# Norm boundaries cut into five token tiles, keys and queries of attention staged under the last projection, three mixing chunks split under the last attention unit

## What is computed

```python
def trunk_layer(x, mod, g_mix_pre, g_mix_post, g_ffn_pre, g_ffn_post, w_ffn_in, w_ffn_conv, w_ffn_out, mixer):
    shift1, scale1, gate1, shift2, scale2, gate2 = mod      # six vectors, silu(c) @ w_mod + b_mod
    h = rmsnorm(x, g_mix_pre) * (1 + scale1) + shift1
    y, ctx_state = mixer(h)                                  # w_in, heads, w_out
    x = x + gate1 * rmsnorm(y, g_mix_post)
    h = rmsnorm(x, g_ffn_pre) * (1 + scale2) + shift2
    x = x + gate2 * rmsnorm(conv_ffn(h, w_ffn_in, w_ffn_conv, w_ffn_out), g_ffn_post)
    return x, ctx_state
```

## Time and profile before

| what | us |
|---|---|
| three runs, median | 1647.64 |
| three runs, lowest and highest | 1643.89, 1649.33 |
| profiled execution, its own time | 1646.06 |
| profiled execution, span | 1644.3 |
| PE busy | 1555.4 (95% of the span) |
| VectorE busy | 1087.6 (66%) |
| ScalarE busy | 700.5 (43%) |
| GpSimd busy | 117.2 (7%) |

### The profile page before, as it was taken

One profiled execution on the slowest core, in us unless ns is written; L12 is line 12 of the kernel. 1 busy time (PEld: TensorE's weight loads), 2 busy tenths in 40 slices (PEclk: granted clock), 3 DMA queues, 4 the chain that ended last, 5 costly groups with the idle time before them and its releaser, 6 DMA issues.

```text
span 1644.3 us, 27983 instructions
## 1 busy us (share of the span) xinstructions
PE 1555.4 (95%) x10553; PEld 1414.5 (86%) x10553; DVE 1087.6 (66%) x2082; ACT 700.5 (43%) x1263; POOL 117.2 (7%) x128
## 2 busy tenths in 40 slices
PE   6799898989999999999989989989899999999997
PEld 2699687879998789998779988768799988999986
DVE  5598766888777867778884248872866641466544
ACT  6631666354443234443252237662644432344332
POOL 1250220000000000000010032410000000000000
PEclk8799899999999999999989989999999999999999
DMA  8234101613334763334642220102222222222222
GB/s 328 105 115 129 33 2 59 211 52 105 113 115 147 217 174 115 115 105 168 198 135 69 75 81 2 44 4 76 61 82 77 70 71 89 73 70 76 70 81 92
DMA packets 45953, 164.54 MB, mean 100 GB/s; under 512 B 5584, under 2 KB 6608, under 8 KB 45104
## 3 DMA queue, kind: packets, MB, share of 16 engines
q1 hardware_dynamic: 42336, 152.00, 28.5%
q0 software_dynamic: 2320, 10.54, 2.0%
q10 hardware_dynamic: 1216, 0.92, 0.2%
HBM read 159.87 MB, written 3.57 MB: 99 GB/s over the span
## 4 chain that ended last, share of the span: by engine, by line
PE 81%; DVE 7%; DMA 2%; issue 2%; ACT 1%; ACTq 0%; DVEq 0%; SPq 0%
PE ps L1842 22%; PE ps L1843 22%; PE ps L1943 13%; PE ps L1935 6%; PE ps L2100 4%; PE ps L2129 4%; PE ps L2042 3%; PE ps L2115 3%; DMA work<-in_wmodt 2%; DVE work L1081 1%; PE ps L1867 1%; PE ps L2034 1%; PE ps L2116 1%; PE ps L2134 1%; DVE product L1081 1%
## 5 line engine op out<-in xcount | busy, mean ns | idle before, releaser
L1842 PE MATMUL ps<-hh,whi 128*128 128x320 f32 x864 | 268.4, 311 | 7.7 <-DVE wlo L1067 3.8
L1842 PE MATMUL ps<-hh,wlo 128*128 128x320 f32 x864 | 267.7, 310 | 0.0
L1843 PE MATMUL ps<-hh,wlo 128*128 128x320 f32 x864 | 267.6, 310 | 0.0
L1842 PE MATMUL ps<-hl,whi 128*128 128x320 f32 x864 | 267.6, 310 | 0.0
L1843 PE MATMUL ps<-hl,whi 128*128 128x320 f32 x864 | 267.6, 310 | 0.0
L1843 PE MATMUL ps<-hh,whi 128*128 128x320 f32 x864 | 267.6, 310 | 0.0
L618 ACT ACTIVATE whi<-raw 128x1024 fp32r<-128x1024 f32 (+1 forms) x112 | 117.0, 1046 | 319.8 <-PE ps L1843 286.8
L612 ACT ACTIVATE whi<-raw 128x1024 fp32r<-128x1024 f32 (+1 forms) x70 | 72.1, 1033 | 264.3 <-PE ps L1943 173.6
L1943 PE MATMUL ps<-whi,ffh 128*128 128x512 f32 x440 | 171.9, 391 | 3.4 <-DVE wlo L1067 2.6
L1067 DVE TENSOR_TENSOR wlo<-raw,whi 128x1024 fp32r<-128x1024 f32 (+1 forms) x72 | 87.5, 1216 | 131.8 <-ACT whi L612 128.6
L1943 PE MATMUL ps<-wlo,ffh 128*128 128x512 f32 x440 | 171.3, 389 | 0.0
(11 more groups left out here) (226 smaller groups left out, 2897.8 us busy)
## 6 DMA issues: line engine op xcount, KB each, us to landing
raw<-in_w SPq DMA_DIRECT2D x174, 512.0 KB, 3.5
work<-in_wmodt SPq DMA_DIRECT2D x56, 512.0 KB, 3.6
ring<-in_wmodt SPq DMA_DIRECT2D x24, 512.0 KB, 4.3
work<-in_wmod SPq DMA_DIRECT2D x16, 512.0 KB, 6.8
grow<-gate_rows POOLq DMA_DIRECT2D x4, 1024.0 KB, 5.8
work<-in_rpb POOLq DMA_DIRECT2D x8, 448.0 KB, 4.5
x<-in_x SPq DMA_DIRECT2D x5, 512.0 KB, 7.9
out_x<-x SPq DMA_DIRECT2D x5, 512.0 KB, 2.6
```

The costliest lines, as they stand in the source:

```text
L1842: T.matmul(bankA[s], slot(w, s, k), h[:, k, 0:HT], start=st, stop=sp_)
L1843: last = T.matmul(bankB[s], slot(w, s, k), h[:, k, HT:NT], start=st, stop=sp_)
```

## The change

Four groups of edits.

1. **Boundaries.** `affine` is called for halves of four chunks, spread over VectorE and ScalarE by two tables. `boundary` becomes `mix_boundary` and `fout1_boundary`; PE turns three tiles and then multiplies tile by tile: ten pieces, five tiles of 128 tokens by two slots. `piece` waits only for its own slot and tile. The hand-written orders of ScalarE and VectorE change with it.
2. **Entries of attention.** Layer 0: the two value units are multiplied one after the other, each over four of the eight k chunks (`value_half` in place of `pair_v`; the host lays the weights out for it); the pooling products stand earlier (`pool_out`); the first keys are split before the last unit, the second ones (`second_keys`) after the first two units' maxima. Layer 1: the last projection signals at k == 3 (`s_free`), and keys and queries are staged from there; VectorE's next low weights stand inside attention. The buffers of the keys are laid out anew.
3. **Start of mixing.** The first three of eight chunks are split (`mix_in_hi`, `mix_in_low`) once all scores are done; the third tile of PE's first chunk waits for the last unit's output.
4. **Chunk loads.** Loads of modulation chunks 24 to 79 move from SP's queue to GpSimd's, with semaphores `s_mlate`; the second `spread_gate` stands behind the load of chunk 55 in that queue.

```diff
 
 
 def width_of(u):
@@ -149,6 +153,11 @@
...
-                if u == 23:
-                    sp.wait_ge(s_tl, 5)
-                if u == 45:
-                    sp.wait_ge(s_ffl, FH + 1)
-                if u == 79:
-                    sp.wait_ge(s_ffl, 2 * FH + 1)
                 for m in LOAD_AFTER.get(u, ()):
-                    sp.wait_ge(s_mused, chunk_before(m) + 1)
-                    chunk_in(m, chunk_buffer(m), ring0 if m < 24 else ring1)
+                    if m < 24:
+                        sp.wait_ge(s_mused, chunk_before(m) + 1)
+                        chunk_in(m, chunk_buffer(m), ring0)
...
-                    act.wait_ge(s_tl, 5 * b + 1)
+                if t >= 2:
+                    act.wait_ge(s_tl, 5 * b + t - 1)
                 st = stream(t)
-                for k in range(KD):
+                for k in range(4 * half, 4 * half + 4):
                     last = nc.scalar.activation(hft[t % 2][:, k, :], turn_bank(t)[:, tile(k)], ACT.Identity,
                                                 scale=coef[:, layer, which, st, k:k + 1],
                                                 bias=mod_col(layer, 0 if which == 0 else 3, st)[:, k:k + 1])
...
             nc.scalar.activation(hst, token_sums[:, :, 0:16], ACT.Sqrt, bias=EPS).then_inc(s_fstd, 1)
-            value_pair(5, v0, 0)
+            for c in range(2):
+                act.wait_ge(s_otp, c + 1)
+                nc.scalar.activation(y[:, c, 0:NS], pooled[c], ACT.Copy, scale=pscale[:, c:c + 1]).then_inc(s_pf, 1)
+                nc.scalar.activation(y[:, c, NS:NT], pooled_prompt[c], ACT.Copy,
+                                     scale=pscale[:, c:c + 1]).then_inc(s_pf, 1)
+            act.wait_ge(s_kn, 2)
+            act.wait_ge(s_unit, 11 + 2)
+            act.wait_ge(s_ctx, 32)
+            nc.scalar.activation(high_keys("B", 0), qk[:, 0, :], ACT.Copy).then_inc(s_kh, 1)
+            hi(12)
+            act.wait_ge(s_unit, 12 + 2)
+            nc.scalar.activation(v0[:, 0:2, :], ps[:, 0, :], ACT.Copy).then_inc(s_fa, 2)
+            act.wait_ge(s_kn, 4)
+            nc.scalar.activation(high_keys("B", 1), qk[:, 1, :], ACT.Copy).then_inc(s_kh, 1)
+            hi(13)
...
-                act.wait_ge(s_oe, (30, 70)[layer])
+                act.wait_ge(s_oe, (5, 45)[layer])
+                act.wait_ge(s_sc, (60, 140)[layer])
                 for c in range(KD):
+                    if c == 3:
+                        act.wait_ge(s_oe, (30, 70)[layer])
                     nc.scalar.activation(hh[:, c, :], y[:, c, :], ACT.Copy).then_inc(s_oth, 1)
...
                                            mod_col(layer, 0 if which == 0 else 3, st)[:, k:k + 1], ALU.mult, ALU.add)
@@ -1309,8 +1359,14 @@
                     rows = qk[:, i, src:src + w]
                     V.tensor_tensor(rows, rows, key_inverse[i][:, f:f + w], ALU.mult).then_inc(s_kn, 1)
             mod_chunk(9, 1, 7, ring0, cwide0, product0)
+            dve.wait_ge(s_kh, 1)
+            V.tensor_tensor(low_keys("B", 0), qk[:, 0, :], high_keys("B", 0).bitcast(F32), ALU.subtract).then_inc(s_kl, 1)
             mod_chunk(10, 0, chunks_loaded(10), ring0, cwide0, product0)
-            value_pair(5, v0, 0)
+            lo(12)
+            mod_chunk(11, 1, chunks_loaded(11), ring0, cwide0, product0)
+            dve.wait_ge(s_unit, 12 + 2)
+            V.tensor_copy(v0[:, 2:4, :], ps[:, 1, :].rearrange("p (t n) -> p t n", t=2))
+            V.tensor_copy(v0[:, 5, :], ps[:, 2, 0:2 * P]).then_inc(s_fb, 2)
...
-            def attention(layer):
+            def attention(layer, meanwhile):
                 units = UNITS_OF[layer]
                 for unit in units[0:2]:
                     for job in unit:
                         neg_max(job)
+                meanwhile()
                 for i, unit in enumerate(units):
                     copy_turned(unit)
                     invert(unit)
                     if i + 2 < len(units):
                         for job in units[i + 2]:
                             neg_max(job)
+                    if i + 1 == len(units):
+                        for c in range(3):
+                            mix_in_low(layer, c)
                     take_values(unit)
-
-            def prepare_attention(n, slots):
-
...
+            def second_keys():
+
+                dve.wait_ge(s_kh, 2)
+                V.tensor_tensor(low_keys("B", 1), qk[:, 1, :], high_keys("B", 1).bitcast(F32),
+                                ALU.subtract).then_inc(s_kl, 1)
+                lo(13)
+
...
+                inverse_x(b, 2)
                 norm_x(b, 1)
-                affine(b, 0)
+                affine(b, 0, 0)
+                affine(b, 1, 1)
+                norm_x(b, 2)
                 lo(u)
                 h_lo(b, 0)
-                inverse_x(b, 2)
                 lo(u + 1)
+                inverse_x(b, 3)
                 gate_mixed(b, 1, 4)
-                norm_x(b, 2)
-                inverse_x(b, 3)
                 norm_x(b, 3)
+                inverse_y(b, 4)
                 h_lo(b, 1)
...
+                if i == 4:
+                    dve.wait_ge(s_kh, 3)
+                    V.tensor_tensor(low_keys("C", 2), qk[:, 12, :], high_keys("C", 2).bitcast(F32),
+                                    ALU.subtract).then_inc(s_kl, 1)
...
+                if i < 4:
+                    lo(u + 2)
                 if i == 0:
...
             spread_gate(0, 0, 1)
-            pool.wait_ge(s_yf, 10)
-            pool.wait_ge(s_coef, 8)
-            spread_gate(1, 0, 3)
+            pool.wait_ge(s_tl, 5)
+            for m in range(24, 80):
+                pool.wait_ge(s_mused, chunk_before(m) + 1)
+                if m == 36:
+                    pool.wait_ge(s_ffl, FH + 1)
+                if m == 67:
+                    pool.wait_ge(s_ffl, 2 * FH + 1)
+                b = chunk_buffer(m)
+                pool.dma_start(ring1[b], a["wmodt"][m]).then_inc(s_mlate[b], 16)
+                if m == 55:
+                    pool.wait_ge(s_yf, 10)
+                    pool.wait_ge(s_coef, 8)
+                    spread_gate(1, 0, 3)
...
                         T.matmul(bankA[s], slot(w, s, k), h[:, k, 0:HT], start=st, stop=sp_)
                         last = T.matmul(bankB[s], slot(w, s, k), h[:, k, HT:NT], start=st, stop=sp_)
+                    if tell_half and k == 3:
+                        last.then_inc(s_free, 1)
...
+            def value_half(u, fu):
+
+                s = u % 2
+                pe.wait_ge(s_lo, u + 1)
+                pe.wait_ge(s_fa, fu - s + 2)
+                pe.wait_ge(s_fb, fu - s + 2)
+                for kk in range(4):
+                    k = 4 * s + kk
+                    for t in range(5):
+                        out = ps[:, t // 2, t % 2 * 2 * P:(t % 2 + 1) * 2 * P]
                         for n, (w, h) in enumerate(((whi, hh), (whi, hl), (wlo, hh))):
-                            last = T.matmul(out, h[:, k, t * P:(t + 1) * P], w[:, :, k * P:(k + 1) * P],
-                                            start=k == 0 and n == 0, stop=k == KD - 1 and n == 2)
-                    if t == 2 and between is not None:
-                        between()
-                last.then_inc(s_unit, 2)
+                            last = T.matmul(out, h[:, k, tile(t)], w[:, s, kk * 2 * P:(kk + 1) * 2 * P],
+                                            start=k == 0 and n == 0 and t % 2 == 0,
+                                            stop=k == KD - 1 and n == 2 and (t % 2 == 1 or t == 4))
+                last.then_inc(s_unit, 1)
...
+                    if half == 0 and t == 2:
+                        pe.wait_ge(s_oe, (30, 70)[layer])
...
-            def piece(u0, c0, c1, bank, f, start, final):
-
-                for s in range(2):
-                    for k in range(KD):
-                        for n, (w, h) in enumerate(((whi, hh), (whi, hl), (wlo, hh))):
-                            last = T.matmul(ps[:, 2 * s + bank, f:f + c1 - c0], slot(w, s, k), h[:, k, c0:c1],
-                                            start=start and k == 0 and n == 0, stop=final and k == KD - 1 and n == 2)
-                    if c1 == NT:
-                        last.then_inc(s_unit, 1)
-
-            def boundary(b, u0):
+            def piece(b, u0, s, t):
 
                 yi = TOKEN_PHASES.index(NORMED[b])
-                for t in range(4):
-                    turn(b, t)
-                pe.wait_ge(s_lo, u0 + 2)
-                pe.wait_ge(s_yf, 10 * yi + 5 + 3)
-                pe.wait_ge(s_afa, 2 * b + 1)
-                pe.wait_ge(s_tl, 5 * b + 2)
-                piece(u0, 0, HF, 0, 0, True, True)
+                pe.wait_ge(s_lo, u0 + s + 1)
+                pe.wait_ge(s_tl, 5 * b + t + 1)
+                if t == 0 and s == 0:
+                    affine_done(pe, b, 1)
+                if t == 0 and s == 1:
+                    pe.wait_ge(s_yf, 10 * yi + 5 + 3)
+                if t == 2 and s == 1:
```

(72 more changed lines are left out.)

237 lines of the change are left out of this document (125 added, 112 removed).

## The result

The changed kernel takes 1710.3 us (median of 4 runs, 1701.38 to 1722.01), the kernel before 1647.76 us (4 runs, 1643.89 to 1649.33): ratio 1.0387, 95% interval 1.0308 to 1.0467. It is slower, as forecast, but by 62.5 us where some 8 were forecast, and outside the range. The profiled execution took 1701.38 us with a span of 1699.6, 55.3 more than before. The runs of the changed kernel lie 20 us apart, and their mean granted clocks run with the times: 0.954, 0.953, 0.942 and 0.939 for 1701.38, 1702.79, 1717.82 and 1722.01.

The account below looks back on a forecast made before the run. TensorE (PE), busy 95% of the span, was taken as the bound. Terms 17.6 - 1.0 - 2.4 - 7.6 - 4.5 + 4.0 + 2.3 = +8.4 us gave about 1655.5 us, range 1646 to 1665.

Parts of the forecast that it names:

- half-clock term of the boundaries: Each norm boundary: after PE's stand, products run briefly at half clock, costing 0.9 us.
- the third: Rival: clock falls at starts of mixing too, or gate rows' write stalls units: +4.4 or +4.5 us, chance 0.15.
- The count of narrow products: Norm boundaries: 240 products of 128 columns each at 0.111 us, 26.6 us instead of 16.8, +9.8 each.
- Rival 2: Boundaries: narrow products cheaper than counted; at 0.081 us each 21 us lower, 1634.6; chance 0.09 including other gains' upper bounds.
- the walk: Boundaries: queues followed with traced durations; in the first, PE begins products near 347.6, 5.6 us earlier than before.
- Entries and starts of mixing: Attention entries save 1.0 us (layer 0) and 2.4 us (layer 1); the two starts of mixing save 7.6 us.
- The step that the clock holds at 1.0: Starts of mixing: shorter waits keep the clock at 2.4 GHz, part of -7.6 us; -3.2 if it falls.
- Chunk loads on GpSimd: Feed-forward output phases: later gate rows -4.5 us, slower loads +4.0 in the first phase and +2.3 in the second.
- rival 1: Chunk loads from GpSimd cost nothing more, all else as forecast: +2.1 us, 1649.7, chance 0.22.
- the ring: First feed-forward's output: VectorE and chunk loads alternate over two buffers; 0.45 us more per link, five links +2.25.
- Rival 4: VectorE holds up GpSimd's load issue by up to 1.2 us at seven links: up to +8, 1663; chance 0.08.

Follow-up runs that it names:

- x2: The kernel before, with each boundary piece of 256 columns issued as two of 128, nothing else changed; 1695.02 us, ratio 1.0289.
- x9: The changed kernel with 16 more float32 transposes of the identity behind the third tile's eight in each boundary; 1657.64 us, ratio 1.0057.
- x3: The changed kernel with its new orders, but PE multiplying boundary pieces of 256, 256 and 128 columns; 1640.26 us, ratio 0.9966.
- x4: The changed kernel with 512-column float32 products filling PE's stands in the boundaries, the 240 narrow products kept; 1653.77 us, ratio 1.0040.
- x6: x1 with the loads of modulation chunks 24 to 79 back in SP's queue and the gate rows at their old place; 1637.91 us, ratio 0.9931.
- x1: The changed kernel with the three norm boundaries put back as before on all engines; 1632.65 us, ratio 0.9919.
- x5: The changed kernel with four 512-column float32 products ahead of the fourth tile's transposes in each boundary, stands left; 1687.33 us, ratio 1.0227.

## Why the prediction was wrong

**The step that failed** is the half-clock term of the boundaries, "0.9 for products at the half clock" in each. I took it from the earlier trace rows, where the old kernel spends 3.6 us at 0.50 after its stand, and carried that over to a boundary in which the 16 transposes in a row (349.50 in the earlier trace rows) are cut to 8 and the products behind them to 128 columns. Those two things were what brought the level back: 16 transposes in a row did it in x2 and 24 in x9, products of 256 columns in x3 and, behind 8 transposes, in the second boundary of the kernel before. The rows allowed the question: the term had a length (3.6 us) and no reason. Measured in its place: 11.8, 28.8 and 54.5 us at the low level. At 0.2135 in place of 0.111 us each, 48% of these 95.1 us are lost, 45.6; the 61.7 less the 16.4 that x4 shows at full level are 45.3. It was outside all my rivals; the third had the clock fall at the starts of mixing, not in the boundaries.

**The count of narrow products was right.** Forecast 5.7 + 6.2 + 5.7 = 17.6 at 0.111 us each with 2.7 for the clock; x4 has 5.3 + 6.1 + 5.0 = 16.4 with the level kept up and some fill in it. Rival 2, 0.081 us each, is out: they took 0.111 to 0.112 at full clock in the changed kernel, x4 and x9. Pieces begin 6.7, 8.9 and 6.7 us behind the token phase in place of 11.8, 12.7 and 11.8, close to the walk (5.6 earlier forecast, 5.1 measured; 4.1 and 3.8 between the layers); the price of the narrow form eats it.

**Entries and starts of mixing**: forecast -1.0, -2.4 and -7.6, together -11.0. By phases of the two traces it is -3.2 to the end of the first mixing and -7.8 from the second boundary to the end of the second, together -11.0 too. That it agrees so closely is luck: the forecast was -4.2 for the first part and -6.8 for the second, and the two misses of 1.0 cancel. In the first mixing PE gains the clock and then waits 1.2 us for VectorE's gated output (L1187), where it did not before. The medians bear the sum out: x6 has 1637.91 us against 1647.17 for the kernel before on the same chip, -9.3 (by its ratio, -11). The step that the clock holds at 1.0 was right.

**Chunk loads on GpSimd**: forecast -4.5 + 4.0 + 2.3 = +1.8. In the changed kernel the stretch that they act on, from the first boundary's end to the second's start, takes 458.2 us against 455.4 before, +2.8, and each term shows in it. The stand of 2.8 us behind the gate rows and the low level after it are gone. The stand for the low weights ahead of 565.35 is 4.1 us in place of 2.2, and the clock falls behind it, as forecast (first row; the second row is x1, where it does not fall):

```profile
565.00:568.30 3.30, 2.95 (x7) 2.37 (x8) 3.30 (x6) 0.00 (x0) 0.42 (x1) 0.50 0.74 267
551.00:558.00 7.00, 4.87 (x21) 4.03 (x22) 7.00 (x11) 0.52 (x1) 1.05 (x2) 1.00 0.61 191
```

In the second output phase there is a new stand of 2.3 us, with a fall of the clock behind it. But this stretch has the same program in eight kernels with the loads on GpSimd, and it took 452.4 (x1), 454.0, 454.5, 455.4, 455.8, 455.9, 455.9 and 458.2 us (the changed kernel); with the loads on SP it took 455.4 (before), 457.3 (x6) and 457.4 (x2). On the mean the move gains 1.4 us, less than the spread of either kind. x1, with a stand of 2.8 us and no fall of the clock, is the best of the eight, and the 4.9 us between it and x6 are not the price of the move. In the other seven the stand is 3.2 to 4.6 us and the clock falls. So the terms are right in kind, the sign of their sum is not settled, and neither is the choice between the forecast and rival 1 (loads from GpSimd cost nothing more). A link of the ring costs about 0.3 us more (6.5 in place of 6.2 from one load's start to the next in x1 and before), where I took 0.45, and nearly all of it is the later start (0.28 against 0.02). Rival 4 (issue held up by VectorE for up to 1.2 us) shows at no link of the chain, in x1 or in the changed kernel.

**Sum by what is measured**: 16.4 + 45.3 - 11.0 = +50.7; with the 2.8 more in layer 0's feed-forward and 1.8 behind the third boundary, where the first dense products still run at the low level, it is the 55.3 of the spans.

**Two slips of the working.** 1647.64 + 8.4 is 1656.0, not 1655.5. And the stand ahead of 349.50 is 6.3 us; the 6.5 of the earlier trace rows belongs to the third boundary. Neither matters.

The Trainium skill, "TensorE: Matmul & The Clock Gate", Part 1, says that activity releases the low level and that the time of activity counts, not the number of products. The trace does not agree if a narrow product counts as activity: 54.5 us of unbroken narrow products stayed at 0.50. Rows of transposes and wide products did release it.

**What stays open.** Why a row of float32 transposes of 128 columns lifts the level and a row of narrow products does not: they differ in type and in operation, and no run tells the two apart. Nor is it settled why 8 transposes amid narrow products lifted the level twice (first and second boundary of the changed kernel) and failed in four other places (three in the changed kernel, one in x2). That this is where the 20 us between its runs come from is likely and not shown, for only one of the runs has a trace: the mean clocks go with the times, and with the rise put at a fixed place the runs lay 3 us apart (x5) and 4 us (x9).

## What to carry to other kernels

Before cutting products into narrower ones to start them earlier, look at the granted clock where they would start: behind stands like these (2.2 and 1.1 us, between the layers 2.7 and 2.6) they may run at half speed for their whole length, and the stand saved is small change against it. If they must be narrow, put a row of transposes or a few wide products between the stand and them, or fill the stand. None of these made the narrow form pay here: x4, x5 and x9 are all slower than x1, which kept the wide pieces. And ask of each stretch at the low level in a profile not only how long it is but what ended it, for a change may take exactly that away.

## What was not expected of the hardware

Products of 128 columns, each behind its own weight load, left PE at 1.2 GHz for 54.5 us without a gap (0.2135 us each), and ran at 2.4 GHz for whole boundaries when they began there (0.111 us each). 24 float32 transposes in a row brought the level back within 3.8 us in three of three places, wide products in every place looked at. A 512 KB load issued by GpSimd landed in 3.9 us in the median, 0.3 us later than from SP, and on the chain it started 0.28 us after its buffer was released, where SP took 0.02. The same stretch of program took 452.4 to 458.2 us in eight kernels that differ only elsewhere.
